# Input sums on three engines, half-rounded weights behind interleaved pairs, and a cache copy cut in eight, in a one-core decoder layer

## The reference

```
u = rms_norm(x) * g * (1 + scale) + shift        # three times; scale, shift, gate = silu(c) @ w_ada + b_ada
h = x + 0.5 * gate0 * swiglu(u0)                 # w_gu1: 1024 x 5632, w_dn1: 2816 x 1024
q, kv, gates, conv, merge gates = u1 @ w_in      # 39 blocks of 128 columns
o = NSA attention (compressed, selected, window) # prompt and samples; the samples read a paged cache
merged = g0 * (o @ w_nsa_out) + g1 * (conv @ w_conv_out)
h = h + gate1 * (merged @ w_out)
y = rms_norm(h + 0.5 * gate2 * swiglu(u2)) * g_final
kv_win_sample = last 512 rows of (window cache + 4 new rows)   # 508 rows of each sample are kept as they are
```

## Time and profile before

| | us |
|---|---|
| three runs | 1464.78, 1466.45, 1473.83 |
| median | 1466.45 |
| profiled execution | 1466.5 |
| its span in the trace | 1464.7 |
| PE busy | 1395.6 (95%) |
| ACT, DVE, POOL busy | 431.8, 533.9, 130.4 |

### The profile page before, as it was taken

One profiled execution on the slowest core, in us unless ns is written; L12 is line 12 of the kernel. 1 busy time (PEld: TensorE's weight loads), 2 busy tenths in 40 slices (PEclk: granted clock), 3 DMA queues, 4 the chain that ended last, 5 costly groups with the idle time before them and its releaser, 6 DMA issues.

```text
span 1464.7 us, 25985 instructions
## 1 busy us (share of the span) xinstructions
PE 1395.6 (95%) x10792; PEld 1288.9 (88%) x10792; DVE 533.9 (36%) x1082; ACT 431.8 (29%) x727; POOL 130.4 (9%) x141
## 2 busy tenths in 40 slices
PE   5799999999999998999889999989899999999996
PEld 1688888999999998999888777879799999999996
DVE  0532222223221215435455635544533333332323
ACT  1412222222211114222224455531434343421111
POOL 4100000000010101000002210033300000001110
PEclk9899999999999999999999999999899999999998
DMA  9347666544442322634444110052132222223321
GB/s 352 128 158 273 216 216 216 166 137 150 144 129 76 104 77 89 197 127 127 125 141 179 44 44 30 23 208 87 44 101 86 86 86 86 86 65 91 85 83 69
DMA packets 97081, 180.52 MB, mean 123 GB/s; under 512 B 13685, under 2 KB 47093, under 8 KB 96158
## 3 DMA queue, kind: packets, MB, share of 16 engines
q1 hardware_dynamic: 96990, 179.23, 37.5%
HBM read 173.07 MB, written 10.28 MB: 125 GB/s over the span
## 4 chain that ended last, share of the span: by engine, by line
PE 88%; DVE 3%; DMA 3%; SPq 2%; issue 1%; ACT 1%; POOL 1%; POOLq 0%; DVEq 0%; ACTq 0%
PE PS L1656 64%; PE PS L1930 6%; PE PS L1590 4%; PE PS L1671 3%; PE PS L1626 2%; PE PS L1944 2%; PE PS L1956 2%; PE PS L1972 2%; SPq L647 1%; DMA raw<-in_w_out 1%; DVE wl L1116 1%; DMA toep_g<-scr_toep 1%; POOL ssq L749 1%; DMA h<-in_xT 1%; ACT wh L815 1%
## 5 line engine op out<-in xcount | busy, mean ns | idle before, releaser
L815 ACT ACTIVATE wh<-raw 128x1024 fp32r<-128x1024 f32 (+2 forms) x215 | 203.4, 947 | 801.7 <-PE PS L1656 761.2
L1116 DVE TENSOR_TENSOR wl<-raw,wh 128x1024 fp32r<-128x1024 f32 (+2 forms) x215 | 241.0, 1121 | 532.5 <-ACT wh L815 532.0
L1656 PE MATMUL PS<-uh,wh 128*128 128x272 f32 x1680 | 354.5, 292 | 6.0 <-DVE wl L1116 3.6
L1656 PE MATMUL PS<-uh,wl 128*128 128x272 f32 x1680 | 348.8, 289 | 0.0
L1656 PE MATMUL PS<-ul,wh 128*128 128x272 f32 x1680 | 347.6, 288 | 0.0
L1656 PEld LDWEIGHTS PS<-uh,wh 128*128 128x128 f32 x1680 | 264.7, 189 | 33.2 <-issue 27.8
L1656 PEld LDWEIGHTS PS<-ul,wh 128*128 128x128 f32 x1680 | 265.2, 189 | 0.0
L1656 PEld LDWEIGHTS PS<-uh,wl 128*128 128x128 f32 x1680 | 263.5, 190 | 0.0
L1656 PE MATMUL PS<-hh,wh 128*128 128x272 f32 x704 | 147.3, 290 | 1.8 <-DVE tmp L1208 0.9
L1656 PE MATMUL PS<-hh,wl 128*128 128x272 f32 x704 | 145.7, 288 | 0.0
L1656 PE MATMUL PS<-hl,wh 128*128 128x272 f32 x704 | 145.1, 288 | 0.0
(11 more groups left out here) (257 smaller groups left out, 1459.1 us busy)
## 6 DMA issues: line engine op xcount, KB each, us to landing
raw<-in_w_gu SPq DMA_DIRECT2D x88, 512.0 KB, 3.5
ada<-in_w_ada SPq DMA_DIRECT2D x32, 1024.0 KB, 5.7
raw<-in_w_in SPq DMA_DIRECT2D x39, 512.0 KB, 3.6
raw<-in_w_dn SPq DMA_DIRECT2D x32, 384.0 KB, 3.2
raw<-in_w_dn SPq DMA_DIRECT2D x32, 320.0 KB, 2.9
ch<-in_cmp_pages SPq DMA_DIRECT2D x64, 128.0 KB, 2.4
kv<-in_sel_pages SPq DMA_DIRECT2D x128, 64.0 KB, 2.0
ada<-in_w_ada_t SPq DMA_DIRECT2D x8, 512.0 KB, 4.1
```

What stands on the lines that cost most here:

```text
L815: e.activation(wh[:, u % SPLITS, 0:n, :], raw[:, u % RAWS, 0:n, :], ACT.Copy).then_inc(hi_ready, 1)
L1116: e.tensor_tensor(wl[:, u % SPLITS, 0:n, :], raw[:, u % RAWS, 0:n, :], f(wh[:, u % SPLITS, 0:n, :]), ALU.subtract).then_inc(lo_ready, 1)
L1656: ins = mm(o[:, a, :], w[:, u % SPLITS, k, :], x[:, k0 + k, HT * a:HT * a + HT], start=(first and k == 0 and w is wh and x is xh), stop=(l ...
```

## The change

Four things. **(1)** x comes in two transfers. GpSimd sums the squares of tiles 0 to 3, ACT squares tiles 4 to 7, DVE adds these. PE does the column sums after three modulation steps instead of five, and the spreading after four instead of six. **(2)** At the middle of each pair PE counts up `pair_half`; the first half of the k-tiles of the next unit is then rounded (`split_first`, `lo_first`), the second half when the pair's first unit is used up. The unit behind a pair waits for each half by itself. **(3)** The copy `win_old` becomes eight transfers, one behind each of the last eight loads of merge-gate weights. **(4)** The scores of attention job 1 stand behind the second half of the merge-gate unit that they stood ahead of.

```diff
+PAIRS = (U_GU1, U_WIN, U_CO, U_GU2)
...
 (SyncE)
-            e.dma_start(h[:, :, :], d["xT"]).then_inc(x_in, 16)
+            for half in range(2):
+                ks = slice(4 * half, 4 * half + 4)
+                e.dma_start(h[:, ks, :], d["xT"][:, ks, :]).then_inc(x_in[half], 16)
...
             for x in range(2 * KD):
                 load(U_MG + x, d["w_in"][23 + x])
+                if x >= KD:
+                    e.dma_start(d["win_old"][x - KD], d["win_src"][x - KD]).then_inc(win_sent, 16)
...
             for m in range(KD):
                 load(U_NSA + m, d["w_no"][m])
-            e.dma_start(d["win_old"], d["win_src"]).then_inc(win_sent, 16)
...
 (GpSimd, sum_squares)
                 if n == 0:
-                    e.wait_ge(x_in, 16)
+                    e.wait_ge(x_in[0], 16)
+                    for k in range(4):
+                        e.wait_ge(ssq_ready, 1 + k)
+                        e.tensor_tensor(sq[:, :], h[:, k, :], h[:, k, :], ALU.mult).then_inc(sq_ready, 1 if k < 3 else 4)
+                        e.wait_ge(sq_ready, 1 + k)
+                        e.tensor_tensor(ssq[:, :], ssq[:, :], sq[:, :], ALU.add).then_inc(ssq_ready, 1 if k < 3 else 4)
+                    return
...
 (ScalarE)
+            def split_first(u):
+                p, n = PAIRS.index(u - 2), unit_k(u) // 2
+                e.wait_ge(raw_in[u % RAWS], 16 * (u // RAWS + 1))
+                e.wait_ge(pair_half, p + 1)
+                e.activation(wh[:, u % SPLITS, 0:n, :], raw[:, u % RAWS, 0:n, :], ACT.Copy).then_inc(hi_half, 1)
+
+            def split_second(u):
+                n = unit_k(u) // 2
+                e.wait_ge(unit_used, u - SPLITS + 1)
+                e.activation(wh[:, u % SPLITS, n:2 * n, :], raw[:, u % RAWS, n:2 * n, :], ACT.Copy).then_inc(hi_ready, 1)
...
 (ScalarE, end of norm)
                 rounded(KD - 1)
+                split_first((U_GU1, U_WIN, U_GU2)[n] + 2)
...
-            square(0)
+            e.wait_ge(x_in[1], 16)
+            for k in range(4, KD):
+                e.activation(work(k), h[:, k, :], ACT.Square).then_inc(x_sq, 1)
             root(0)
...
             for m in range(KD):
-                split(U_CO + m + 2)
+                if m:
+                    split(U_CO + m + 2)
+                else:
+                    split_first(U_CO + 2)
+                    split_second(U_CO + 2)
...
 (VectorE, end of norm)
+                lo_first((U_GU1, U_WIN, U_GU2)[n] + 2)
                 e.wait_ge(u_lo, 8 * n + KD)
...
+            e.wait_ge(x_sq, 2)
+            e.tensor_tensor(rinv[:, :], work(4), work(5), ALU.add).then_inc(x_sum, 1)
+            for k in (6, 7):
+                e.wait_ge(x_sq, k - 3)
+                e.wait_ge(x_sum, k - 5)
+                e.tensor_tensor(rinv[:, :], rinv[:, :], work(k), ALU.add).then_inc(x_sum if k == 6 else sq_last, 1)
             e.wait_ge(vec_in, 16)
...
+            lo_first(U_CO + 2)
             for m in range(KD):
                 e.wait_ge(unit_used, U_CO + m + 1)
...
 (TensorE, unit)
-                e.wait_ge(lo_ready, u + 1 + more)
+                halved = isinstance(more, int) and u - 2 in PAIRS
+                if halved:
+                    e.wait_ge(lo_half, PAIRS.index(u - 2) + 1)
+                else:
+                    e.wait_ge(lo_ready, u + 1 + more)
                 for k in range(n):
+                    if halved and k == n // 2:
+                        e.wait_ge(lo_ready, u + 1)
...
 (TensorE, two_units)
                         if k == nk - 1:
                             ins.then_inc(unit_used, 1)
+                        elif k == nk // 2 - 1 and v == 1:
+                            ins.then_inc(pair_half, 1)
...
-            for k in range(5):
+            for k in range(3):
                 ada_step(k)
             norm_sum(0)
-            ada_step(5)
+            ada_step(3)
             norm_spread(0)
-            ada_step(6)
-            ada_step(7)
+            for k in range(4, KD):
+                ada_step(k)
...
             s_step(1, 9)
+            fill(KD // 2)
             for s in range(GQ):
                 p_score(1, s)
-            fill(KD // 2)
```

More of the change, by code:

```diff
@@ L315, in build @@
         toep_out = sem("toep_out")
-        x_in = sem("x_in")
+        x_in = [sem(f"x_in{half}") for half in range(2)]
+        x_sq = sem("x_sq")
+        x_sum = sem("x_sum")
         cond_in = sem("cond_in")
@@ L343, in build @@
         unit_used = sem("unit_used")
+        pair_half = sem("pair_half")
+        hi_half = sem("hi_half")
+        lo_half = sem("lo_half")
         psum_free = sem("psum_free")
@@ L860, in tile @@
                     e.activation(dst, tmp[:, fi % 2, :], ACT.Copy).then_inc(hid_hi, 1)
+                tile(0)
                 with e.Fori(0, KF // 2 - 1) as i:
-                    tile(0, i)
                     tile(1, i)
-                tile(KF - 2)
+                    tile(2, i)
                 tile(KF - 1)
@@ L1117, in lo, with lo_first, lo_second @@
                                 ALU.subtract).then_inc(lo_ready, 1)
+            def lo_first(u):
+                p, n = PAIRS.index(u - 2), unit_k(u) // 2
+                e.wait_ge(hi_half, p + 1)
+                e.tensor_tensor(wl[:, u % SPLITS, 0:n, :], raw[:, u % RAWS, 0:n, :], f(wh[:, u % SPLITS, 0:n, :]),
+                                ALU.subtract).then_inc(lo_half, 1)
+            def lo_second(u):
+                n = unit_k(u) // 2
+                e.wait_ge(hi_ready, u + 1)
+                e.tensor_tensor(wl[:, u % SPLITS, n:2 * n, :], raw[:, u % RAWS, n:2 * n, :],
+                                f(wh[:, u % SPLITS, n:2 * n, :]), ALU.subtract).then_inc(lo_ready, 1)
             def inv_root(n):
@@ L1437, in _ @@
                     s_step(*SAMPLE_AT[n])
-                lo(U_WIN + n + 2)
+                if n:
+                    lo(U_WIN + n + 2)
+                else:
+                    lo_second(U_WIN + 2)
                 if n >= 11:
```

37 lines of the change are left out of this document (26 added, 11 removed).

## The result

The changed kernel takes 1454.11 us (median of 6 runs, 1451.67 to 1457.25) where the kernel before took 1465.62 (6 runs, 1462.43 to 1473.83): ratio 0.9914, 95% interval 0.9895 to 0.9932. Timed again beside other runs of the kernel before it was 1453.31 (1450.99 to 1456.85), ratio 0.9901 (0.9881 to 0.9920). So, by the two ratios, 12.6 to 14.5 us were gained where 16.4 were forecast; the forecast time of 1450.1 was 4.0 under the measured one. The profiled execution, 1457.25, is the slowest of its six; against the profiled one of before it gained 9.25.

The account below looks back on a forecast made before the run. TensorE is 88% of the chain that ended last, so edits pay only where it idles or runs at low clock. Gains at the places touched sum to 16.4, taken from 1466.5 to give 1450.1 us; range 1445 to 1457.

Parts of the forecast that it names:

- Start, 4.0: Kernel start: modulation copied out 4.0 us earlier, bound by the last modulation weights and steps; gain 4.0 (3.1 to 4.6).
- The collision that I weighed against it: At the start, DVE's three adds contend with POOL and end at 23.8, not 20.4; the start then gains 3.1.
- Gaps behind the pairs: Behind the four pairs, halved rounding shortens PE's waits: gains 0.44, 1.97, 0.33 and 1.98 us, first to fourth.
- Copy, 5.5: Output projection: without the whole copy ahead of its weights, the last k-tile starts 5.5 us earlier (4.5 to 6.3).
- The bound chosen for the new kernel: Output projection: the chain making the last activation tile, ACT's then DVE's rounding, limits; last k-tile about 7.2 us behind attention output.
- The pieces: Copy pieces between 798 and 881, behind loads whose weights are rounded 45 us later or more: costed at nothing.
- Clock behind the second pair, 1.75: Behind the second pair, at 576 to 579: with no gap, the low-clock stretch goes; gain 1.75 us (0 to 1.75).
- the clock stretch turns up elsewhere: Rival: the low-clock stretch behind the second pair stays or appears at another place; 1451.9 us, chance 0.20.
- Moved scores, 0.4: First attention jobs: the chunk fills PE's wait for the bias, steady run starts 0.4 us earlier (minus 2.4 to 0.7).
- DVE's order starts from the same landing: First attention jobs: DVE's operations still start from the bias landing at 781.3, so PE transposes at 785.6 instead of 786.13.
- The rival that the moved scores lose: First attention jobs: slower chunk, DVE's second bias behind it; 0.4 not gained, up to 2.4 lost, 1452.9 us, chance 0.06.
- The low ends of the terms: The smallest gain allowed for each place; the prediction said the ends of all terms give 1446 to 1455 us.

Follow-up runs that it names:

- experiment 4: Kernel before, with none of the change, but PE kept busy in its gaps by unread matmuls: 1459.66 us; the same with the change: 1446.05.
- warm: Changed kernel with two compression products moved into the second pair's norm gap, plus unread matmuls at start, first pair and fourth pair's norm: 1446.05 us.
- warm_best: Changed kernel with all these gaps filled by unread matmuls, job 1's scores in the old order, three more filling calls during the bias wait: 1442.64 us.

## Why the prediction was right, and where not

- **Start, 4.0:** right in size (3.95, 4.15) and in mechanism, each time at its place. The collision that I weighed against it did not come: DVE's adds run from 17.83, POOL ended at 17.3. About half of the 4 us was clock (1.9 are left where both kernels keep PE busy, experiment 4), which the sum had in it through the durations at 1.2 GHz.
- **Gaps behind the pairs:** second 1.97 forecast, 2.06 measured (3.61 less the stretch of 1.55); first 0.44, 0.5 with the clock held (0.19 and 1.23 in the two executions of the changed kernel, without and with the stretch gone); third 0.33, 0.26; fourth 1.98, measured 1.99 on PE (2.23 from the last weight to the next unit, now 0.24) and some 0.6 more in small steps up to 1320, whose cause I didn't look for.
- **Copy, 5.5:** 5.76 to 5.80 in all nine traces that have it, but each time against the one profiled execution of before, which was the dearest of five; against the other four it is 3.8 to 5.7 (its growth of 5.77 in the lead between 800 and 992.8, less what those four gain there without it). The bound chosen for the new kernel was the right chain, with 7.1 instead of 7.2 us to the last k-tile. The pieces cost nothing that shows.
- **Clock behind the second pair, 1.75:** the step failed in kind. The stretch was in one of three executions of that program (in two of five traces with the same gap of 1.81), so its removal is worth 1.55 in some and nothing in others. I had read it, and the 1.00 of the norm and of the first jobs, as properties of the kernel. In the first jobs the profiled execution of before was the exception: of the 13 other traces only warm and warm_best ran at 1.00. In the norm it was not (1.00 in all traces without the start's shift), and there the change itself may have a part. By its time it was on the quiet side as well, though not by much: 19 of 63 executions are at or under 1466.5. I gave the rival *the clock stretch turns up elsewhere* 0.20 and 1.8 us. It came true at two places at once, for 3.4 us and, together with the moved scores, about 3 in the profiled execution, and at one of them, for about 1, in the second.
- **Moved scores, 0.4:** the sign was wrong. The step that failed is "DVE's order starts from the same landing", hence transposes at 785.6, 4.2 behind the read. Measured 5.99, because DVE's chain took 6.33, not 4.67. I had counted what the chunk does for PE and not that its end releases POOL's two additions, 1.33 each, into DVE's chain. What it costs is 1.2 to 1.7 where 0.4 were to be gained. The rival that the moved scores lose named another reason (the chunk slower), and the collision of DVE and POOL was looked for at the start and in the output projection, not here.
- **Queue:** ahead of unit 9 the earlier kernel finds SP still issuing pages (9.6 to 10.4 us for 16), and the raw weights late: between 582 and 640 0.7 of the lead was lost in the first execution, 1.6 in the second, at most 0.2 with PE kept busy. I had left out this margin. Waits over the whole span, us, times, longest, against the earlier trace rows:
```profile
ACT wh L832 <- DMA raw<-in_w_in: 24.3, 3, 9.8
```

The parts measured one by one add up to 16.4 by their ratios (5.4 + 5.3 + 7.3 - 1.6), the number that was forecast. That is luck: the moved scores are in it with minus 1.6 instead of 0.4, and intervals of 2 to 3 us on each part leave some 5 us on the sum. The kernel with all but the moved scores gained 16.3 where the other terms add up to 16.0. Of the 2 to 4 us by which the whole change fell short, 1.6 to 2.1 are the moved scores. The rest, up to 2, is no more than the noise of these comparisons; low clock at places where the one trace of before had none would account for it, and how much of that a median execution pays stays open.

Two terms were also taken from an execution that had their places at their dearest (the copy, and the stretch behind the second pair), and the first jobs, which it had at their cheapest, were taken as free. These errors go against each other, so that the time came out as near as 4 us is in part luck. The low ends of the terms add up to 9.9 us, which is 1456.6 and not the 1455 that I wrote; the range of 1445 to 1457 held the time because the rivals had been let in.

## What to carry to other kernels

A granted clock below 1.00 in one trace can be a draw and not a property of the kernel: before it enters a sum, or before its absence does, the same program has to be seen more than once, or the mean clock of the timed runs compared with that of the profiled one. The same holds for a wait behind a large transfer, here 3.1 to 5.3 us. Where PE's idle gaps are known and useless matmuls fit into them, these can be worth as much as shaving gaps (6.3 us here, from 1452.37 to 1446.05), and they narrow the spread, so that small edits can be measured at all. And when an edit lets an engine finish earlier, ask what its end releases: here two additions of POOL, let into the middle of DVE's chain.

## What the runs showed of the hardware that was not expected

- **Executions differ by the clock.** Of 63 executions of the kernel before, the 23 with a mean granted clock of 0.980 or more took 1463.3 to 1467.1 us, the 13 at 0.976 or less 1468.6 to 1473.5. With the gaps filled the mean clock is 0.994 in the best version's profile, and its five runs lie within 2.9 us.
- **A low clock comes behind some gaps every time and behind others now and then.** Behind the gap of 3.6 us ahead of the first pair and that of 3.8 us ahead of the fourth it was there in all nine traces that leave them open. Behind the same gap of 1.42 us PE ran at 0.56 in one execution of a program and at 1.00 in the next; in the first attention jobs 11 of 14 traces had it. Useless matmuls of 0.26 us each (two for one call) lifted both pairs to 1.00.
- **Some of DVE's operations wait for POOL's to end.** Two operations of 0.17 took 0.92 and 1.08, and ended 0.01 to 0.02 behind POOL's additions; the rounding of 2.38 in the earlier trace rows started at 986.43, in an addition of POOL from 985.96 to 987.73, and ended 1.08 behind it, nearly its whole free time of 1.23. A reciprocal of 0.18 within the same addition was not held up. The Trainium skill, SBUF — State Buffer, section *SBUF: two separate sides*, says that the pair of ports that DVE and GpSimd share is "an exclusive lock, not a bandwidth split". The traces of the held operations agree: a collision cost them what was left of POOL's instruction (0.75 and 0.91 us here), and not a share of their own time.
